# Turns between stages by token tile with a late scale, gathers for two expert pairs, and a last expert matrix loaded by halves of its columns

## The chip, the cores and the metric

One Trainium2 chip, of which the kernel uses one core. The metric is the device time of one execution in microseconds. PE is TensorE (matmul), ACT ScalarE, DVE VectorE, POOL GpSimd, SP the engine that issues the loads. SBUF is the on-chip memory, PSUM the eight banks that TensorE writes.

## The reference

Three layers over S = 256 tokens of width D = 1024, all in fp32. Layers 0 and 1 are each attention and a gated FFN with a convolution of three taps over the tokens (MLA attention in layer 0, differential attention in layer 1). The third has block and index attention and a mixture of 32 experts, two of which each token takes.

```python
# layers 0 and 1
a = rms_norm(h, norm_g[i, 0]);  a = mla_mixer(...) or diff_mixer(...)
h = h + rms_norm(a, norm_g[i, 1])
f = conv_ffn(rms_norm(h, norm_g[i, 2]), ...)   # up 1024 -> 2 x 2816, conv, gelu(g) * val, down
h = h + rms_norm(f, norm_g[i, 3])
# third layer: attention as above, then for each expert e and the tokens routed to it
hid = jax.nn.silu(xb @ w1[e]) * (xb @ w3[e])   # 1024 -> 512
ys = hid @ w2[e]                               # 512 -> 1024
```

rms_norm(x, g) is x * rsqrt(mean(x*x) + eps) * g, for each token.

## The kernel before

Tokens are held in two tiles of 128 (t = 0, 1): `h` and `xn` are 128 x 2 x 1024 in SBUF. The weights of layers 0 and 1 and of the third layer's attention come as pieces of 2048 columns through a ring of four raw buffers. ACT makes the high fp32r part of a piece (L1281), POOL the low part (`lows`, L611), and PE forms three fp32r products of each pair of operands (L649 to L651: high by high, low by high, high by low). A piece therefore passes SP, ACT and POOL before PE, in this order. Each engine runs a program of its own, in order, held together by semaphores. Instructions of one engine don't pass each other, so the place of an instruction in it is the schedule.

A stage's output goes to the next at a **turn**. There are four: from the MLA output projection to the FFN of layer 0 (turn 1, next input `x1`), from there to the differential attention (turn 2, `x2`), from that to the second FFN (turn 3, `x3`), and on to the third layer (turn 4, `x4`). In `post` DVE multiplies each of the four PSUM banks by the gain into `xn` (L1758), while ACT sums the squares (L1292), forms one scale for both tiles (L1764, then L1306 on ACT and L1683 to L1691 on DVE) and adds the scaled rows to `h` (L1770). At turns 1 to 3 ACT then squares `h`, DVE forms the next scale and writes `xn` with it (`normed`, L1734); PE transposes `xn` (L659), ACT copies the high part (L1323) and DVE makes the low part (L1710). At turn 4 the next scale isn't applied to `xn` (`x_gained`, L1746): it is put in as a row behind the first products. Meanwhile PE runs 32 matmuls that nobody uses, so that its clock stays up:

```python
WAIT = 32
```

In an FFN tile ACT centres the PSUM bank of the up product with its first tap and bias (L1458), DVE adds the other taps (L1931, L1936), ACT and DVE form the gelu, and DVE leaves the high and low hidden parts (L1945, L1947); PE uses them some tiles later in the down product. ACT splits the next piece between these steps.

In the expert stage 32 experts are taken in 16 pairs, 64 slots to an expert. Each expert has three matrices of 2 MB, which stay fp32 and come through slots of SBUF that earlier stages leave (`four_pairs`, L565 to L590; SP waits on `slots_used`). Per pair PE does w1 and w3 (L1211), the selection's transposes, the gather of the next pair's tokens (L1163), the transposes of the hidden part (L1222), w2 (L1237), and the scatter of the pair before (L1193). The gather multiplies `xn` with a 0/1 matrix `Sel` that DVE makes from the tokens' positions in their expert (L2197), and DVE copies it out (L2205). The last pair's w2 is loaded in two parts of its rows k.

## Time and profile before

| | us |
|---|---|
| median of 3 runs | 1363.15 |
| lowest and highest run | 1363.07, 1370.86 |
| profiled execution, its own time | 1361.37 |
| its span | 1359.6 |
| PE busy | 1285.8 (95%) |
| ACT busy | 549.0 (40%) |
| POOL busy | 568.2 (42%) |
| DVE busy | 510.5 (38%) |
| bytes moved | 341.22 MB |

The mean granted clock of PE was 0.992. The time is some 1.8 us more than the span of the engines' work. The three thirds of the span differ: up to 880 us the engines share the work of split weights, from about 906 us the transfers stand at 428 GB/s with POOL idle, and the last 25 us are the end of the last pair and the final norm. Parts of the page give shares over the whole span; the stretches are seen in the windows and timelines.

### The profile page before, as it was taken

How to read it: one execution, taken by the hardware profiler on the slowest of the kernel's cores; microseconds unless marked ns; L12 is line 12 of the kernel's file. 1: busy time of each engine (PE TensorE's matmuls, PEld its weight loads, DVE VectorE, ACT ScalarE, POOL GpSimd, SP SyncE). 2: the span in 40 equal slices, each digit the busy share in tenths (PEclk: the TensorE clock that was granted, in tenths of full speed). 3: DMA queues.
4: the chain of work that ended last, by engine and by line, in shares of the span. 5: the costliest groups of instructions: out<-in, count | busy, mean ns of one | idle time of the engine just before them, and what ended most of it. 6: DMA issues, size and time to landing. Idle time of an engine off the chain costs nothing.

```text
span 1359.6 us, 20047 instructions
## 1 busy us (share of the span) xinstructions
PE 1285.8 (95%) x7971; PEld 958.3 (70%) x7971; DVE 510.5 (38%) x1307; ACT 549.0 (40%) x853; POOL 568.2 (42%) x132
## 2 busy tenths in 40 slices
PE   6999999999998899999999899999999999999996
PEld 5867899998986799999877788854445444454442
DVE  2334544445265454444657264431112111121113
ACT  4544655556477465555544465221111111111112
POOL 5532788885954188888568555400000000000000
PEclk9999999999999999999999899999999999999998
DMA  7622566654633176665446443599999999999994
GB/s 268 216 81 89 154 199 200 190 187 154 217 124 94 62 213 190 186 185 172 154 147 201 135 145 128 208 422 426 429 429 428 428 428 430 429 430 429 429 427 176
DMA packets 154821, 341.22 MB, mean 251 GB/s; under 512 B 8473, under 2 KB 119418, under 8 KB 142202
## 3 DMA queue, kind: packets, MB, share of 16 engines
q1 hardware_dynamic: 154746, 340.18, 67.2%
q8 instruction: 53, 0.87, 0.3%
q14 instruction: 22, 0.18, 0.0%
HBM read 339.10 MB, written 1.05 MB: 250 GB/s over the span
## 4 chain that ended last, share of the span: by engine, by line
PE 72%; DMA 15%; DVE 5%; ACT 4%; POOL 2%; issue 2%; SPq 0%; ACTq 0%; DVEq 0%
PE bank L649 16%; PE bank L651 15%; PE bank L650 15%; DMA ring<-in_w 10%; PE bank L1211 10%; PE bank L1237 5%; DMA xspare<-in_w 4%; PE bank L1163 2%; PE bank L748 2%; POOL parts L611 2%; PE bank L659 1%; ACT parts L1281 1%; PE bank L1193 1%; PE bank L1097 1%; PE bank L782 1%
## 5 line engine op out<-in xcount | busy, mean ns | idle before, releaser
L611 POOL TENSOR_TENSOR parts<-raw,parts 128x2048 fp32r<-128x2048 f32 (+4 forms) x128 | 568.0, 4465 | 305.5 <-ACT parts L1281 305.5
L649 PE MATMUL bank<-xh,parts 128*128 128x256 f32 x1032 | 289.0, 280 | 12.1 <-ACT room L1318 5.9
L650 PE MATMUL bank<-xl,parts 128*128 128x256 f32 x1032 | 286.7, 278 | 0.0
L651 PE MATMUL bank<-xh,parts 128*128 128x256 f32 x1032 | 286.6, 278 | 0.0
L1281 ACT ACTIVATE parts<-raw 128x2048 fp32r<-128x2048 f32 (+4 forms) x128 | 235.9, 1853 | 33.1 <-PE bank L649 18.0
L1211 PE MATMUL bank<-ring,room 128*64 128x512 f32 x768 | 226.2, 594 | 8.6 <-DMA ring<-in_w 5.8
L649 PEld LDWEIGHTS bank<-xh,parts 128*128 128x128 f32 x1032 | 194.5, 189 | 18.9 <-issue 10.6
L650 PEld LDWEIGHTS bank<-xl,parts 128*128 128x128 f32 x1032 | 195.3, 189 | 0.8
L651 PEld LDWEIGHTS bank<-xh,parts 128*128 128x128 f32 x1032 | 194.6, 189 | 0.0
L1211 PEld LDWEIGHTS bank<-ring,room 128*64 128x64 f32 x768 | 73.3, 137 | 112.5 <-issue 112.5
L649 PE MATMUL bank<-parts,xh 128*128 128x512 f32 (+5 forms) x304 | 114.6, 377 | 9.6 <-POOL parts L611 2.8
L1237 PE MATMUL bank<-ring,room 128*64 128x512 f32 x384 | 113.3, 595 | 0.7 <-ACT room L1642 0.7
L650 PE MATMUL bank<-parts,xh 128*128 128x512 f32 (+5 forms) x304 | 112.0, 368 | 0.0
L651 PE MATMUL bank<-parts,xl 128*128 128x512 f32 (+5 forms) x304 | 112.0, 368 | 0.0
L1642 ACT ACTIVATE room<-bank 128x512 f32<-128x512 f32 x16 | 9.6, 597 | 193.6 <-PE bank L1222 193.6
L651 PE MATMUL bank<-parts,hl 128*128 128x512 f32 x192 | 75.6, 394 | 0.0
L649 PE MATMUL bank<-parts,hh 128*128 128x512 f32 x192 | 74.6, 389 | 0.8 <-POOL parts L611 0.8
L650 PE MATMUL bank<-parts,hh 128*128 128x512 f32 x192 | 75.3, 392 | 0.0
L1458 ACT ACTIVATE room<-bank,room 128x256 f32<-128x256 f32 x64 | 32.7, 561 | 102.2 <-PE bank L651 101.1
L649 PEld LDWEIGHTS bank<-parts,xh 128*128 128x128 f32 x304 | 57.9, 190 | 22.4 <-issue 4.9
L1318 ACT ACTIVATE room<-bank 128x512 f32<-128x512 f32 (+1 forms) x75 | 41.1, 581 | 77.3 <-PE bank L659 35.2
L1237 PEld LDWEIGHTS bank<-ring,room 128*64 128x64 f32 x384 | 34.5, 137 | 50.2 <-issue 48.0
(255 smaller groups left out, 1804.4 us busy)
## 6 DMA issues: line engine op xcount, KB each, us to landing
ring<-in_w SPq DMA_DIRECT2D x71, 2048.0 KB, 23.1
raw<-in_ffn_w_up SPq DMA_DIRECT2D x88, 512.0 KB, 4.9
room<-in_w SPq DMA_DIRECT2D x12, 2048.0 KB, 20.1
raw<-in_ffn_w_down SPq DMA_DIRECT2D x44, 512.0 KB, 3.9
xspare<-in_w SPq DMA_DIRECT2D x11, 2048.0 KB, 26.8
raw<-in_w_in SPq DMA_DIRECT2D x40, 512.0 KB, 4.2
raw<-in_diff_w_qkv SPq DMA_DIRECT2D x24, 512.0 KB, 4.5
raw<-in_mla_w_o SPq DMA_DIRECT2D x8, 512.0 KB, 4.6
```

Source lines behind the costliest of these rows:

```text
L611: pool.tensor_tensor(low[:, p % PARTS, 0:n], raw[:, p % RING, 0:n], high[:, p % PARTS, 0:n], ALU.subtract).then_inc(low_ready, 1)
L649: first = pe.matmul(out_, a[0], b[0], start=start, stop=False)
L650: pe.matmul(out_, a[0], b[1], start=False, stop=False)
L651: return first, pe.matmul(out_, a[1], b[0], start=False, stop=stop)
L659: ins = pe.transpose(b[0:cols, at:at + rows], src, ident[0:rows, 0:rows])
L748: ins = pe.matmul(b[:, t * S:t * S + S], qs[n][:, t * P:t * P + P], ks[n], start=n == 0, stop=n == len(qs) - 1)
L1163: ins = pe.matmul(bank[2 + k // 4][:, P * (k % 4):P * (k % 4) + P], xn[:, t, P * k:P * k + P], Sel[:, t].rearrange("p e c -> p (e c)"), st ...
L1211: ins = pe.matmul(bank[x][CAP * e:CAP * e + CAP, :], XgT[:, k, CAP * e:CAP * e + CAP], rows_of(j, x, e, k, EF), start=k == 0, stop=k == KT ...
L1237: ins = pe.matmul(bank[1 + hf][CAP * e:CAP * e + CAP, :], hidT[:, k, CAP * e:CAP * e + CAP], rows_of(j, 2, e, k, D)[:, 512 * hf:512 * hf + ...
L1281: act.activation(high[:, p % PARTS, 0:n], raw[:, p % RING, 0:n], ACT.Copy).then_inc(high_ready, 1)
L1318: act.activation(dst, src, func, scale=scale).then_inc(bank_moved[BANK[g]], 1)
L1458: act.activation(fbuf[b][a], bank[b][:, a * S:a * S + S], ACT.Identity, bias=par(3, a), scale=par(1, a)).then_inc(centre, 1)
```

## The change

It has three parts. **The turns** (`turn_over` for `post`, `normed` and `x_gained`): DVE takes the two token tiles one after the other, in halves of 512 columns, each tile with a scale of its own; POOL makes the second halves of `xn`; the next rms scale isn't applied to `xn` at turns 1 to 3 either, but is formed after the transposes, put on the diagonal of a matrix by DVE and turned into a row over all tokens by two small PE matmuls (`scales_in_rows`) behind the first group of products. In the FFN DVE multiplies each up tile in PSUM by this row ahead of the centring; the q and k groups of the differential attention are multiplied by it as they are copied out, by DVE instead of ACT; v takes the scale in ACT's copy. `WAIT` is 8. **The experts**: the rows are split into fp32r high (ACT) and low (DVE), `Sel` holds four experts and is double buffered, and a gather step fills half the rows of the input for two pairs, with 16 fp32r matmuls over 256 columns a pair instead of 16 fp32 ones over 128. **The last w2** is loaded and used by halves of its columns.

In the order of the diff below: POOL's gains, PE's fillers, scale row and gathers, ACT's `x_next`, DVE's `turn_over`, FFN tile and rows' split, and SP's last loads.

```diff
+            def gains(site):
+                pool.wait_ge(gpre_here, 16 * (site + 1))
+                for t in range(NT):
+                    pool.wait_ge(h_ready, 2 * (site - 1) + t + 1)
+                    pool.tensor_tensor(xn[:, t, 512:D], h[:, t, 512:D], gpre[:, 512:D], ALU.mult).then_inc(xn_ready, 1)
+            next_stage = {W[name] + 1: n + 1 for n, name in enumerate(["ffn0", "qkv", "ffn1", "qi"])}
...
-            WAIT = 32
+            WAIT = 8
...
+            def scales_in_rows(n):
+                pe.wait_ge(diag_ready, n)
+                g = G[f"row{n}" if n < 4 else "row"]
+                b = begin(g)
+                for t in range(NT):
+                    ins = pe.matmul(b[:, t * P:t * P + P], cs[:, C_ONE:C_ONE + P], diag[:, t], start=True, stop=True)
...
                 up(b, 0)
+                scales_in_rows(2 * l + 1)
                 up(b + 1, 1)
...
+            def gather(half, at, first, last, sel, b=2, frees=0):
                 for k in range(first, last):
+                    for x in range(2):
+                        for t in range(NT):
+                            row = (row_high[t], rows_r[:, t, :])[x][:, P * (at + k):P * (at + k) + P]
+                            ins = pe.matmul(bank[b + k // 2][:, 2 * P * (k % 2):2 * P * (k % 2) + 2 * P], row,
+                                            Sel[sel][:, t].rearrange("p e c -> p (e c)"),
...
             def one_round(base, fours, first=False, behind=None):
-                gather(base)
+                pe.wait_ge(sel_ready, 2 + base)
+                gather(base, 0, 0, 4, 0)
+                gather(base + 1, 4, 0, 4, 0, b=4)
...
+            def x_next(site):
+                high_tiles(f"x{site}", HALVES, 4)
+                h_sums(site, 28, 8448)
+                if site < 4:
+                    g = G[f"row{site}"]
+                    full(act, g)
+                    if site == 2:
+                        act.activation(late_key_row, bank[BANK[g]][:, 0:S], ACT.Copy, scale=HD_SCALE).then_inc(key_row, 1)
+                    copy(g, late_row, bank[BANK[g]][:, 0:S])
...
+                for t in range(NT):
+                    scale_of(t)
+                    added(t, 0)
+                    dve.tensor_tensor(xn[:, t, part[0]], h[:, t, part[0]], gpre[:, part[0]], ALU.mult).then_inc(xn_ready, 1)
+                for t in range(NT):
+                    added(t, 1)
+                late_scales(name, site + 1)
...
             def tile(n, b, par):
+                dve.wait_ge(up_full, 1 + n)
+                both = bank[b][:, :].rearrange("p (a s) -> p a s", a=2)
+                dve.tensor_tensor(both, both, late_row.unsqueeze(1).to_broadcast([P, 2, S]), ALU.mult).then_inc(rows_put, 1)
...
+            for t in range(NT):
+                dve.wait_ge(rows_high, t + 1)
+                dve.scalar_tensor_tensor(rows_r[:, t, :], xn[:, t, :], st[:, 16 + t:17 + t],
+                                         row_high[t], ALU.mult, ALU.subtract).then_inc(rows_split, 1)
             dve.wait_ge(mask_ready, 1)
...
-                            sp.dma_start(slots[c][:, a * HALF:a * HALF + HALF].unsqueeze(1),
-                                         w[:, bass.ds(8 * i + (2 * j + e), 1), a * HALF:a * HALF + HALF]).then_inc(done[c], 16)
+                            sp.dma_start(r3(slots[c], b=D)[:, :, 512 * a:512 * a + 512],
+                                         A["w2_2"][0].rearrange("e (p k) n -> p e k n", p=P)[
+                                             :, 8 * i + 2 * j + e, :, 512 * a:512 * a + 512]).then_inc(done[c], 16)
```

DVE's program at turn 1, before:

```order
L1758 TENSOR_TENSOR xn<-bank,gpost 128x512 x4
L1764 TENSOR_TENSOR st<-st 128x2
L1683 TENSOR_SCALAR st<-st 128x1 x2
L1688 TENSOR_SCALAR st<-st 128x1 x2
L1691 TENSOR_SCALAR st<-st 128x1 x2
L1770 SCALAR_TENSOR_TENSOR h<-xn,st,h 128x1024 x2
L1683 TENSOR_SCALAR st<-st 128x1 x2
L1688 TENSOR_SCALAR st<-st 128x1 x2
L1691 TENSOR_SCALAR st<-st 128x1 x2
L1734 SCALAR_TENSOR_TENSOR xn<-h,st,gpre 128x512 x4
L1710 TENSOR_TENSOR xl<-bank,xh 128x4x128 x4
```

and now:

```order
L1806 TENSOR_TENSOR xn<-bank,gpost 128x512
L1815 TENSOR_TENSOR st<-st 128x1
L1806 TENSOR_TENSOR xn<-bank,gpost 128x512
L1736 TENSOR_SCALAR st<-st 128x1
L1741 TENSOR_SCALAR st<-st 128x1
L1744 TENSOR_SCALAR st<-st 128x1
L1826 SCALAR_TENSOR_TENSOR h<-xn,st,h 128x512
L1835 TENSOR_TENSOR xn<-h,gpre 128x512
```

The two gains, the scale and half an addition of one tile stand together now; tile 1 repeats the eight rows, and after them come two more halves of `h`, the low parts, and only then the scale of the next norm and its diagonal:

```order
L1826 SCALAR_TENSOR_TENSOR h<-xn,st,h 128x512 x2
L1763 TENSOR_TENSOR xl<-bank,xh 128x4x128 x4
L1736 TENSOR_SCALAR st<-st 128x1 x2
L1741 TENSOR_SCALAR st<-st 128x1 x2
L1744 TENSOR_SCALAR st<-st 128x1 x2
L1789 COPY st<-st 128x2
L1792 TENSOR_SCALAR room<-cs,st 128x128 x2
L1997 TENSOR_TENSOR bank<-bank,room 128x512
L2000 SCALAR_TENSOR_TENSOR room<-bank,convT,room 128x255 x2
```

ACT's program at turn 2 (`x2`), before, from the scale of `h` to the first split pieces:

```order
L1306 ACTIVATE st<-st,eps_t 128x2
L1323 ACTIVATE xh<-bank 128x4x128 x4
L1499 ACT_TABLE_LOAD
L1499 ACTIVATE st<-st 128x2
L1281 ACTIVATE parts<-raw 128x2048 x2
L1318 ACTIVATE room<-bank 128x512
L1281 ACTIVATE parts<-raw 128x2048
L1318 ACTIVATE room<-bank 128x512
```

and now:

```order
L1359 ACTIVATE st<-st,eps_t 128x1
L1376 ACTIVATE xh<-bank 128x4x128 x4
L1345 ACTIVATE room,st<-h 128x1024 x2
L1359 ACTIVATE st<-st,eps_t 128x2
L1550 ACTIVATE prow<-bank 128x256
L1371 ACTIVATE room<-bank 128x256
L1561 ACT_TABLE_LOAD
L1561 ACTIVATE st<-st 128x2
L1334 ACTIVATE parts<-raw 128x2048 x7
```

The squaring of `h` has moved behind the copies of the transposed tiles, the two row copies (L1550, L1371) stand ahead of the table load (L1561), and the seven splits (L1334) stand behind all of them with no copy of q or k between.

DVE's program at the head of the experts, before:

```order
L2177 TENSOR_SCALAR room<-room 128x2
L2182 SCALAR_TENSOR_TENSOR room<-bank,room 128x64
L2184 TENSOR_SCALAR room<-room 128x64
L2185 TENSOR_REDUCE st<-bank 128x1
L2187 TENSOR_SCALAR flag<-st 128x1
L2197 TENSOR_TENSOR room<-cs,room 128x128 x2
```

and now:

```order
L2251 TENSOR_SCALAR room<-room 128x2
L2254 SCALAR_TENSOR_TENSOR rows_r<-xn,st,gains_r 128x1024
L2254 SCALAR_TENSOR_TENSOR rows_r<-xn,st,tables_r 128x1024
L2260 SCALAR_TENSOR_TENSOR room<-bank,room 128x64
L2262 TENSOR_SCALAR room<-room 128x64
L2263 TENSOR_REDUCE st<-bank 128x1
L2265 TENSOR_SCALAR flag<-st 128x1
L2273 TENSOR_TENSOR room_r<-cs,room 128x256 x2
```

The two low parts of the rows (`rows_r`) stand ahead of the positions, and the selection (L2273) is twice as wide.

## Rows read from the trace of the kernel before

**Rows 1.** Page, part 4, the chain that ended last, share of the span by engine.

```profile
PE 72%; DMA 15%; DVE 5%; ACT 4%; POOL 2%; issue 2%; SPq 0%; ACTq 0%; DVEq 0%
```

**Rows 2.** Windows; columns: window, us, busy of each engine, PEclk, DMA share, GB/s.

```profile
210.00:300.00 90.00, 90.00 (x648) 84.09 (x648) 43.12 (x104) 49.36 (x62) 77.11 (x18) 1.00 0.61 190
...
904.00:906.00 2.00, 2.00 (x10) 0.72 (x12) 1.21 (x6) 0.38 (x1) 0.00 (x0) 1.00 0.98 336
906.00:1335.00 429.00, 418.50 (x2268) 200.54 (x2266) 75.75 (x162) 55.07 (x75) 0.00 (x0) 1.00 1.01 428
```

**Rows 3.** The chain that ended last, in order of time; columns: start us, us, what.

```profile
1298.29 31.55 DMA ring<-in_w
...
1339.59 7.11 PE bank L1237 x32
...
1348.07 1.47 DVE h L2232 x3
```

**Rows 4.** Timeline around turn 2, and its last FFN tile; columns: start, us, engine, line, operation.

```profile
315.48 0.42 DVE L1947 TENSOR_TENSOR hl<-bank,hh 128x256 fp32r<-128x256 f32 x1
...
319.27 2.68 DVE L1758 TENSOR_TENSOR xn<-bank,gpost 128x512 f32<-128x512 f32 x4 [3.37 <-ACT room L1292]
...
320.11 7.24 PEld L678 LDWEIGHTS bank<-xh 128*128 128x128 f32 x32
...
323.32 2.48 DVE L1770 SCALAR_TENSOR_TENSOR h<-xn,st,h 128x1024 f32<-128x1024 f32 x2
...
332.29 0.19 PEld L649 LDWEIGHTS bank<-xh,parts 128*128 128x128 f32 x1 [0.80 <-DVE xl L1710]
...
332.38 1.28 ACT L1499 ACT_TABLE_LOAD   x1
...
334.07 3.70 ACT L1281 ACTIVATE parts<-raw 128x2048 fp32r<-128x2048 f32 x2
...
338.25 0.60 ACT L1318 ACTIVATE room<-bank 128x512 f32<-128x512 f32 x1 [0.47 <-PE bank L651]
...
343.90 0.60 ACT L1318 ACTIVATE room<-bank 128x512 f32<-128x512 f32 x1 [3.25 <-PE bank L651]
```

**Rows 5.** Timeline of turn 4.

```profile
651.92 7.25 PEld L678 LDWEIGHTS bank<-xh 128*128 128x128 f32 x32
...
657.52 2.49 DVE L1746 TENSOR_TENSOR xn<-h,gpre 128x512 f32<-128x512 f32 x4
...
662.06 0.19 PEld L649 LDWEIGHTS bank<-parts,xh 128*128 128x128 f32 x1 [0.96 <-DVE xl L1710]
```

**Rows 6.** Timeline of turn 1 and of the FFN's first pieces behind it.

```profile
125.09 7.23 PEld L678 LDWEIGHTS bank<-xh 128*128 128x128 f32 x32
...
143.22 1.02 ACT L1458 ACTIVATE room<-bank,convT 128x256 f32<-128x256 f32 x2 [5.89 <-PE bank L651]
...
150.75 0.38 PE L649 MATMUL bank<-xh,parts 128*128 128x256 f32 x1 [1.92 <-POOL parts L611]
```

**Rows 7.** The widest form of POOL's low parts; count, busy us, mean ns, idle before.

```profile
L611 POOL TENSOR_TENSOR parts<-raw,parts 128x2048 fp32r<-128x2048 f32 x116 | 533.7, 4627 | 277.7 <-ACT parts L1281 277.7
```

**Rows 8.** Timeline of POOL and of DVE around 711.

```profile
708.67 9.67 POOL L611 TENSOR_TENSOR parts<-raw,parts 128x2048 fp32r<-128x2048 f32 x2 [9.08 <-ACT parts L1281]
...
711.20 2.67 DVE L2045 TENSOR_TENSOR score<-score,cs 128x512 f32<-128x512 f32 x1
```

**Rows 9.** Windows where the clock fell, and one where it held.

```profile
449.00:451.00 2.00, 0.87 (x4) 0.69 (x5) 0.75 (x1) 0.29 (x1) 2.00 (x1) 0.97 0.00 0
451.00:453.00 2.00, 2.00 (x6) 1.61 (x5) 0.00 (x0) 0.50 (x2) 2.00 (x1) 0.50 0.00 0
742.00:746.00 4.00, 1.32 (x10) 0.87 (x9) 3.90 (x8) 3.98 (x3) 2.46 (x1) 1.00 0.42 145
```

**Rows 10.** Timeline of the head of the experts.

```profile
891.50 0.22 DVE L2182 SCALAR_TENSOR_TENSOR room<-bank,room 128x64 f32<-128x64 f32 x1 [1.32 <-PE bank L1151]
...
892.91 3.81 PE L1163 MATMUL bank<-room,xn 128*128 128x128 f32 x32 [1.52 <-DVE room L2197]
```

More of the change, by code:

```diff
@@ L249, in build @@
         h = sb("h", [P, NT, D])
+        with nc.sbuf_tensor("rows_r", [P, NT, D], F32R) as rows_r:
+            pass
         xn = sb("xn", [P, NT, D])
@@ L998, in _ @@
             by_token(G["qi"], W["qi"], X, [3, 3, 2], [256, 328])
-            pe.wait_ge(diag_ready, 1)
-            b = begin(G["row"])
-            for t in range(NT):
-                ins = pe.matmul(b[:, t * P:t * P + P], cs[:, C_ONE:C_ONE + P], diag[:, t], start=True, stop=True)
-                if t == 0:
-                    behind(ins)
-            end(ins, G["row"])
+            scales_in_rows(4)
             columns("qa")
@@ L1949, in ffn @@
             def ffn(l):
+                moved(dve, G[f"row{2 * l + 1}"])
                 for j in range(6):
@@ L2219, in pair @@
                                          ALU.mult).then_inc(hidden_ready, 1)
-                if not last:
-                    take(n + 1)
+                if gathers:
+                    take(n + 2, j % 2, (j // 2 + 1) % 2)
                 for hf in range(2):
@@ L2251, in _ @@
             link(ins)
-            link(dve.tensor_copy(gpair, gate[:, :, 0:2]))
-            take(0)
+            gates_of(0).then_inc(gates_put, 1)
+            for half in range(2):
+                take(half, half, 0, 2 + 2 * half)
             dve.wait_ge(flag_ready, 1)
@@ L2262, in _ @@
                     dve.wait_ge(last_added, 4 * r)
-                    select(r * NP, 0)
-                    take(r * NP)
+                    select(0, 0)
+                    gates_of(0).then_inc(gates_put, 1)
+                    for half in range(2):
+                        take(r * NP + half, half, 0, 2 + 2 * half)
                     one_round(r * NP)
```

295 lines of the change are left out of this document (158 added, 137 removed).

## The prediction

> **What bounds the kernel now.** I read the chain that ended last first: TensorE has 72% of it and DMA 15% [rows 1]. The windows say where each holds. In the loops of the conv-FFN TensorE is busy for all 90 of 90 us, in the expert stage (906 to 1335) the DMA share is 1.01 at 428 GB/s [rows 2]. The end of the chain confirms the second: the last w3 of a pair lands at 1329.84 after 31.55 us, and only then TensorE goes on [rows 3]. The expert stage moves 32 experts of 6.3 MB, 201.3 MB; at 428 GB/s that is 470 us, so its length is fixed by when its stream starts and how it ends, not by TensorE. Between the two stand the four turns, where TensorE has only its filler (L678). With T the filler's first weight load, the first product of the next stage follows at T+12.18 in turn 2 (320.11 to 332.29) and T+10.14 in turn 4 (651.92 to 662.06) [rows 4, 5]. Turn 1 has the same T+12.2, but there TensorE runs dry again later: ACT splits the third piece of the FFN only behind the first tile's centring (L1458, 143.22), POOL needs 4.6 us more, and TensorE resumes at 150.75, T+25.7 with T = 125.09 [rows 6]. Turn 3 has the same shape.
>
> **The change, part by part.** All times below are against T of their turn.
>
> *1. The turn's own chain.* Before: four products with the gain, one scale for both tiles, two additions of 1024, two squarings of 1.06 us, a second scale, four xn, transposes [rows 4]. After: DVE does tile 0 to the end, then tile 1. Prices: 0.69 for a 128x512 pass (2.68 us for four), about 1.0 for the sum and scale of one tile (for two they lie between 321.95, where L1758 ends, and 323.32). Turn 2: DVE may start 0.8 before T (L1758 at 319.27). Tile 0: two gains, sum, scale, one half added, one half of xn: until T+2.8. Tile 1 the same again, 3.7: T+6.4 to 6.6. Two more additions: h is ready at T+7.1 and 7.8. Then POOL makes the second halves. It ran no 512-wide pass; 2048 wide took 4.63 us [rows 7], a quarter is 1.16, and I take 1.3 with something for the start. POOL: 7.2 to 8.5 to 9.8. Last transposes (0.66 a set) end at T+10.5, and the product begins there, since its first half of the tiles has been ready long since. I add 0.3 for DVE and POOL holding each other up, so T+10.8 in turns 2 and 4. Turns 1 and 3 have squares 1.4 us earlier: T+9.4.
>
> That 0.3 is a choice between 0 and 0.7. The row for it: an addition of 128x512 with both inputs in SBUF took 2.67 us at 711.20 while a POOL pass ran from 708.67 on [rows 8], and the same form takes 0.62 in turn 4, where POOL stands still [rows 5]. In the new turn POOL's two passes overlap at most the last addition and the first low parts, so one instruction can be late by up to half a POOL pass.
> The Trainium skill (SBUF — State Buffer, Who interferes with whom) says that a DVE instruction with two SBUF inputs contends with a GpSimd instruction that reads SBUF, and that whoever issues first keeps the shared ports for its whole length; this trace agrees, 2.67 against 0.62 us. By that rule and the estimate of 1.3 us a pass the sum would gain up to 1.3 us more per turn.
>
> *2. The fillers.* Eight instead of 32: they end at about T+2.1 instead of T+7.7. After that TensorE has only sets of four transposes in 6 to 7 us. What such a hole does stands in the windows: at 449:451 TensorE was busy 0.87 of 2 us, and at 451 the granted clock went to 0.50, the lower of its two levels; in 742:746, busy 1.32 of 4, it held [rows 9]. Either may follow the new holes. A fall costs what the half-speed stretch of some 3 to 3.5 us withholds, less what was idle in it: 0.2 to 1.9 us. I take 1.0 for each turn, as the chance of it is above even.
>
> *3. Turns 1 and 3.* Here the third piece decides, not the first product. First group of products: T+9.4, 5.9 long as in turn 2 (332.29 to the copy at 338.25), plus 1.0 of clock: T+16.3. Now the scale row stands between it and the centring: row product 0.5, ACT's copy 0.65, DVE's multiplication of the tile in PSUM 0.7; then centre 0.95, split 1.9, POOL 4.6. Sum: T+25.6, against T+25.7. Worth 0 each (-1.6 if the clock holds). What the shorter chain wins, the row and the multiplication spend.
>
> *4. Turn 2.* ACT's work behind it sets the end again, by a new order: all seven splits now stand behind both row copies, and behind the table load. T+10.8, first group 5.65, clock 1.0, row product 0.75: 18.2. Two copies 0.8, table and exp (1.28 and 0.2) 1.5, split 1.9, POOL 4.63: T+27.0. Before, the two splits of L1281 began at 334.07, within the first group, and the third group could start at T+12.2+2x5.65 = T+23.5. Worth +3.5 (+2.0 without the clock and the 0.3; +4.5 with more idle in a half-speed stretch).
>
> *5. Turn 4.* It had the late scale already, and a T of 10.14. After: 10.8 plus 1.0, so +1.6 (0 to +2.7).
>
> *6. The FFN tiles.* 44 multiplications of 0.69 us on DVE, 30 us of work. In the loops DVE is busy 43 of 90 us and TensorE all of it, so they cost nothing if the delay of 0.7 to 0.8 a tile fits. The tightest place is the last tile, which nothing follows: its low part is done at 315.90, and its twelve products of 0.23 us (L678: 7.24 for 32) end where the filler begins, at 320.3 [rows 4], so begin at 317.6. Slack 1.7: it fits. If the cover were gone, 44x0.7 is 31 us.
>
> *7. Head of the experts.* DVE's two new splits of the rows (128x1024, two SBUF inputs, 1.25 each by L1770) stand ahead of the positions, on which select and gather wait. DVE was idle for 1.32 us ahead of L2182 and hides that much of the 2.5: +1.2 [rows 10]. Select is 256 wide instead of 128: +0.4. Gather: 16 fp32 matmuls (32 records, two for each) took 3.81 us; two half gathers of 16 products over 256 columns, at the 0.117 us of such a product in the FFN (48 between the copies at 338.25 and 343.90, 5.65 us), are 1.87 each. They begin at 892.91+1.2+0.4 = 894.5 and end at 898.2; the experts' first product, at 896.7 before, comes 1.5 later. TensorE's idle ahead of the gather grows from 1.5 to about 2.9 us: another possible fall of the clock, +1.0 (0 to 1.7). Does the stream feel it? The loads that follow go into the room that the first matrix leaves, about 7 us behind the gather, and at 904:906 the rate is 336 GB/s [rows 2]: the stream is nearly dry there, so a later first matrix passes one to one. +2.5.
>
> *8. Gathers of two pairs.* 1.9 us a pair less on TensorE. A pair's 12.6 MB take 29.4 us at 428 GB/s, and TensorE was busy 418.5 of 429 us, at most 28.7 of each 29.4: it waits already, and with 1.9 less it waits longer: 0.
>
> *9. Last matrix by halves of columns.* Its first half now ends earlier, but the additions to h queue behind DVE's second low part and started at 1348.07 [rows 3]. Gain 0 to 0.3, I take 0.2. Rows of 2 KB instead of 8 KB could slow the load. By 428 GB/s its 4.2 MB end some 9.8 us behind the w3 before it, at 1339.7, and the second half is wanted half of L1237's 7.11 us after 1339.59, at 1343.1: 3 us of cover, 0.
>
> Sum: 0 + 3.5 + 0 + 1.6 + 2.5 - 0.2 = +7.4. The profiled execution took 1361.37, 1.8 below the median of 1363.15, so it would be 1368.8 there; on the median's scale 1370.5, which I round to 1370.
>
> **The rivals.**
> *A, the clock holds* in the turns and at the head, and contention costs nothing: -1.6-1.6+2.0+0+1.5-0.2 = +0.1: 1363. For it: 742:746 held. Against: 449:451 did not.
> *B, the turns' chain gains more* than I count (POOL's passes overlap better, ACT gets ahead of the table load): each turn 2 us shorter than forecast, 1355 to 1358. Faster by under 1%.
> *C, TensorE bounds the expert stage*: then 14 to 16 pairs by 1.9 give -27 to -30: about 1336 to 1340. Against it stands a DMA share of 1.01 over 429 us.
> *D, the FFN's multiplication is exposed.* It decides once the chain from a full bank to its low part (centre, convolution, gelu on ACT and DVE alternately) exceeds the slack of two tiles. Beyond it each 0.3 us a tile costs 13: 1380 to 1395.
>
> **How the numbers follow.** About 1% (13.6 us) is what a measurement of this kernel can tell from no change. Forecast 0.58, A 0.18, B 0.09, C 0.04, D and like stalls 0.11. Cases A, B and the forecast lie within 1%, but the forecast's upper end (all clock terms at 1.9, turn 2 at 4.5) reaches 1377: a little of it is slower. Faster 0.06, same 0.80, slower 0.14. The range leaves out C, D and part of B: 1358 to 1378.
>
> **What would show it.** Turn 2: first product at T+10.8 and a wait of TensorE for POOL's low part before the third group, ending at T+27; ACT's first split after the table load. Turns 1 and 3: resumption at T+25.6. PEclk at half in each turn. The first expert product 1.5 to 2.5 us later against the head's start, DMA share 1.01 behind it, and TensorE's wait per pair longer by 1.9. Wrong if TensorE idles between FFN tiles, if the experts' stream falls below 428 GB/s, or if no wait for POOL follows turn 2.

## The result, and the profile after

The change makes the kernel slower. The median is 1381.55 us (1380.13 to 1382.94, 4 runs) against 1363.11 (1361.99 to 1370.86); the ratio is 1.0135, 95% interval 1.0107 to 1.0162. The forecast was 1370, so about 7 of the 18 us were seen, and the rest was not. The interval excludes a difference of under 1%.

The page of the changed kernel, its first line, and the chain by engine, which answers to [rows 1]:

```profile
span 1379.8 us, 19410 instructions
...
PE 63%; DMA 21%; DVE 7%; ACT 4%; POOL 3%; issue 2%; SPq 0%; ACTq 0%; DVEq 0%; POOLq 0%
```

The cores view: span and mean granted clock. It was 0.992 before:

```profile
core 0: 1379.8 us, clock 0.969
```

The chain has lost TensorE's share to DMA and DVE, and the clock has lost 0.023. Multiplied out, (1 - mean clock) x span x 2 is the time at half speed: 86 us here, 22 before. That is the first thing to see.

Both kernels run the same 4680 split products ahead of the experts, and the same 1024 of w1 and w3 in them. The n-th one of each trace can therefore be set side by side, and the growth of its delay shows where the 20.2 us of span arose:

| place | delay grows by | forecast |
|---|---|---|
| turn 1, with the stretch behind its late third piece | +1.8 | 0 |
| last tile of the first FFN | +1.0 | 0 |
| turn 2 and its q, k and v products | +4.2 | +3.5 |
| differential attention | +4.3 | 0 |
| turn 3, with the stretch behind its late third piece | +0.7 | 0 |
| last tile of the second FFN | +1.0 | 0 |
| turn 4 | +1.1 | +1.6 |
| attention of the third layer | +3.5 | 0 |
| head of the experts | +3.0 | +2.5 |
| experts and end | -0.4 | -0.2 |

Six rows with a forecast of 0 hold 12.3 us. The windows show the other common cause. Columns are window, us, busy of each engine, PEclk, DMA share, GB/s, for the changed kernel:

```profile
131.00:138.00 7.00, 5.67 (x26) 5.27 (x27) 3.14 (x9) 3.63 (x8) 2.39 (x2) 0.52 0.00 0
329.00:336.00 7.00, 5.03 (x22) 4.23 (x23) 4.37 (x7) 2.85 (x6) 2.87 (x2) 0.52 0.28 67
349.00:352.00 3.00, 2.19 (x10) 2.19 (x11) 0.00 (x0) 1.51 (x1) 3.00 (x2) 0.57 0.34 90
414.00:421.00 7.00, 6.06 (x23) 4.86 (x24) 2.85 (x6) 1.72 (x6) 2.96 (x1) 0.52 0.42 120
...
756.00:759.00 3.00, 1.02 (x8) 0.58 (x8) 2.90 (x6) 3.00 (x2) 1.36 (x1) 1.00 0.58 204
760.00:766.00 6.00, 6.00 (x15) 4.65 (x15) 2.53 (x5) 2.74 (x9) 6.00 (x2) 0.51 0.46 149
926.00:1355.00 429.00, 401.75 (x2012) 176.31 (x2010) 73.45 (x146) 55.07 (x75) 0.00 (x0) 0.98 1.01 427
```

There are half-speed stretches in turn 1 (131), turn 2 (329), behind the late pieces (349), in the differential attention (414), and in the third layer's attention (760), where the kernel before kept its clock through the same hole at 742 [rows 9]. Up to the first gather of the experts the trace has thirteen such stretches, the trace of before three. Those three stand ahead of the same products here too (at 442, 462 and 779); ten are new, of which five were forecast. The last row answers to [rows 2]: the expert stage still runs at a DMA share of 1.01, with TensorE busy for 402 instead of 418 of 429 us. What the wider gathers save is idle time.

**Turn 2** in the changed kernel's timeline, which answers to [rows 4]. Its T is the first filler's weight load:

```profile
322.86 1.80 PEld L715 LDWEIGHTS bank<-xh 128*128 128x128 f32 x8
...
330.27 2.87 POOL L642 TENSOR_TENSOR xn<-h,gpre 128x512 f32<-128x512 f32 x2 [6.96 <-DVE h L1826]
...
333.96 0.56 PE L686 MATMUL bank<-xh,parts 128*128 128x256 f32 x1
...
341.14 0.38 ACT L1550 ACTIVATE prow<-bank 128x256 f32<-128x256 f32 x1 [3.80 <-PE bank L840]
...
341.82 1.28 ACT L1561 ACT_TABLE_LOAD   x1
...
343.23 5.50 ACT L1334 ACTIVATE parts<-raw 128x2048 fp32r<-128x2048 f32 x3
...
345.20 18.26 POOL L633 TENSOR_TENSOR parts<-raw,parts 128x2048 fp32r<-128x2048 f32 x4 [12.07 <-ACT parts L1334]
...
349.81 0.58 PE L686 MATMUL bank<-xh,parts 128*128 128x256 f32 x1 [3.25 <-POOL parts L633]
```

The first product comes at T+11.1 (forecast T+10.8), the third group at T+26.95 (forecast T+27.0) behind a wait of 3.25 us for POOL. And ACT stands idle for 3.80 us ahead of the row copies, with two pieces waiting to be split behind them.

**The last tile of the first FFN**, DVE and ACT and then the product that waits:

```profile
313.26 0.42 DVE L2016 TENSOR_TENSOR hl<-bank,hh 128x256 fp32r<-128x256 f32 x1
313.60 0.69 DVE L1997 TENSOR_TENSOR bank<-bank,room 128x512 f32<-128x512 f32 x1
...
314.33 1.02 ACT L1511 ACTIVATE room<-bank,room 128x256 f32<-128x256 f32 x2 [2.36 <-DVE bank L1997]
...
319.75 0.42 DVE L2016 TENSOR_TENSOR hl<-bank,hh 128x256 fp32r<-128x256 f32 x1
...
320.23 0.50 PE L686 MATMUL bank<-parts,hh 128*128 128x512 f32 x1 [0.72 <-DVE hl L2016]
```

The low part that was done at 315.90 before [rows 4] is done at 320.17. Of these 4.3 us, 1.75 is the delay that TensorE has throughout the FFN's loop, so the tile itself is 2.5 us later, against a slack of 1.7. The multiplication takes 0.69 us, but it stands behind the whole of the tile before on DVE, and ACT's centring can't start ahead of it any more.

**The differential attention.** The changed kernel's DVE and PE at one step:

```profile
411.68 0.69 DVE L2044 TENSOR_TENSOR room<-bank,prow 128x512 f32<-128x512 f32 x1 [0.78 <-PE bank L688]
...
414.11 0.69 DVE L2060 TENSOR_TENSOR room<-bank,rs_o 128x512 f32<-128x512 f32 x1
...
414.94 2.05 PE L811 MATMUL bank<-room 128*128 128x128 f32 x8 [2.87 <-DVE room L2060]
```

and the same step before:

```profile
405.83 0.69 DVE L1981 TENSOR_TENSOR room<-bank,rs_o 128x512 f32<-128x512 f32 x1
...
406.66 1.13 PE L774 MATMUL bank<-room 128*128 128x128 f32 x8 [1.59 <-ACT room L1318]
```

DVE now copies a k group out (L2044), and waits for TensorE's own products to do so, ahead of the scale and the scaling of two heads' outputs (L2060). TensorE waits 2.87 us for them, then the clock is at half: its eight matmuls take 2.05 instead of 1.13 us.

**Head of the experts**, which answers to [rows 10]:

```profile
907.71 1.28 DVE L2254 SCALAR_TENSOR_TENSOR rows_r<-xn,st,gains_r 128x1024 fp32r<-128x1024 f32 x1
908.91 1.28 DVE L2254 SCALAR_TENSOR_TENSOR rows_r<-xn,st,tables_r 128x1024 fp32r<-128x1024 f32 x1
910.10 0.22 DVE L2260 SCALAR_TENSOR_TENSOR room<-bank,room 128x64 f32<-128x64 f32 x1
...
911.78 0.36 PE L1212 MATMUL bank<-room_r,gains_r 128*128 128x256 f32 x1 [2.76 <-DVE room_r L2273]
```

The idle time ahead of the gather is 2.76 us (forecast 2.9), and the clock falls at 913, within the gather.

Executions of one kernel differ by more than these terms: the kernel before ran between 1358.0 and 1371.6 in 63 executions. So each verdict below rests on several executions or on a place in a trace, and the text says on which. The changed kernel itself was timed in one set alone; the kernel before had a median of 1361.3 beside e1 to e4, 1363.3 beside e9 to e12 and 1363.2 beside e13 to e16. The four sets of experiments ran on four chips. A distance to the changed kernel's 1381.55 therefore compares two sets, and is uncertain by some 2 us.

### The profile page after: what moved, and what is told of

The parts are those of the page before. It is cut to its first block, busy times and chain, and to the rows that moved or that the text cites. A ratio compares the mean times of both kernels' runs of the same rounds, so it can differ in the third digit from the quotient of the medians.

```text
span 1379.8 us, 19410 instructions
## 1 busy us (share of the span) xinstructions
PE 1269.4 (92%) x7631; PEld 935.6 (68%) x7631; DVE 558.1 (40%) x1358; ACT 546.8 (40%) x853; POOL 579.1 (42%) x140
## 4 chain that ended last, share of the span: by engine, by line
PE 63%; DMA 21%; DVE 7%; ACT 4%; POOL 3%; issue 2%; SPq 0%; ACTq 0%; DVEq 0%; POOLq 0%
DMA ring<-in_w 16%; PE bank L686 15%; PE bank L688 15%; PE bank L687 15%; PE bank L1262 7%; DMA xspare<-in_w 4%; PE bank L1289 3%; PE bank L785 2%; POOL parts L633 2%; ACT parts L1334 1%; PE bank L696 1%; POOL xn L642 1%; PE bank L1212 1%; DVE h L1826 1%; PE bank L1145 1%
## 5 line engine op out<-in xcount | busy, mean ns | idle before, releaser
L686 PE MATMUL bank<-xh,parts 128*128 128x256 f32 x1032 | 293.8, 285 | 15.7 <-POOL parts L633 9.4
L687 PE MATMUL bank<-xl,parts 128*128 128x256 f32 x1032 | 290.4, 281 | 0.0
L688 PE MATMUL bank<-xh,parts 128*128 128x256 f32 x1032 | 290.2, 281 | 0.0
L1334 ACT ACTIVATE parts<-raw 128x2048 fp32r<-128x2048 f32 (+4 forms) x128 | 235.5, 1852 | 49.3 <-PE bank L686 28.4
L1262 PE MATMUL bank<-ring,room 128*64 128x512 f32 x768 | 232.8, 609 | 17.4 <-DMA ring<-in_w 13.1
L686 PEld LDWEIGHTS bank<-xh,parts 128*128 128x128 f32 x1032 | 198.9, 193 | 22.0 <-issue 10.6
L687 PEld LDWEIGHTS bank<-xl,parts 128*128 128x128 f32 x1032 | 198.9, 193 | 0.8
L688 PEld LDWEIGHTS bank<-xh,parts 128*128 128x128 f32 x1032 | 198.5, 192 | 0.0
L1262 PEld LDWEIGHTS bank<-ring,room 128*64 128x64 f32 x768 | 75.5, 140 | 125.1 <-issue 125.1
L686 PE MATMUL bank<-parts,xh 128*128 128x512 f32 (+5 forms) x304 | 116.9, 385 | 8.4 <-DVE room L1867 2.7
L1289 PE MATMUL bank<-ring,room 128*64 128x512 f32 x384 | 113.3, 596 | 1.7 <-DMA ring<-in_w 1.0
L687 PE MATMUL bank<-parts,xh 128*128 128x512 f32 (+5 forms) x304 | 113.9, 375 | 0.0
L1289 PEld LDWEIGHTS bank<-ring,room 128*64 128x64 f32 x384 | 35.1, 137 | 50.9 <-issue 47.5
L2298 DVE SCALAR_TENSOR_TENSOR room<-room,bank 128x512 f32<-128x512 f32 x16 | 18.1, 1128 | 124.2 <-PE bank L1262 124.2
```

The source lines that it names most:

```text
L686: first = pe.matmul(out_, a[0], b[0], start=start, stop=False)
L687: pe.matmul(out_, a[0], b[1], start=False, stop=False)
L688: return first, pe.matmul(out_, a[1], b[0], start=False, stop=stop)
L1262: ins = pe.matmul(bank[x][CAP * e:CAP * e + CAP, :], XgT[j // 2 % 2][:, k, P * (j % 2) + CAP * e:P * (j % 2) + CAP * e + CAP], rows_of(j, ...
L1289: ins = pe.matmul(bank[1 + hf][CAP * e:CAP * e + CAP, :], hidT[:, k, CAP * e:CAP * e + CAP], rows_of(j, 2, e, k, D)[:, 512 * hf:512 * hf + ...
L1334: act.activation(high[:, p % PARTS, 0:n], raw[:, p % RING, 0:n], ACT.Copy).then_inc(high_ready, 1)
```

## The experiments

All but e3, e4, e11 and e12 are edits of the changed kernel.

**e1, 32 fillers again.**

```diff
-            WAIT = 8
+            WAIT = 32
```

> The changed kernel with 32 fillers at each turn again instead of 8 (nothing else). Theory 'clock': a good part of the 20 us lies in stretches at half clock, of which 131 to 138, 328 to 336, 475 to 480 and 670 to 678 begin in the turns after the eight fillers. With 32 the fillers end at T+7.7 and the last two sets of transposes are not due before T+7 to T+10, so these four stretches go away or shrink and the span falls by 3 to 6 us, to 1374 to 1377. Rival 'place in the program': the lost time comes from the order on ACT and DVE; then the span stays within 1 us of 1379.8, or grows by up to 1 us a turn, since the first transposes now queue behind the fillers.

One execution, 1383.7 us, 2.2 more than the changed kernel, not 3 to 6 less. In its trace two stretches at half clock don't belong to the edit, one at 40 us (+1.5) and one at 720 (+3.2, of which 2.2 come back at 760 and 780, where its stretches are shorter). At the turns themselves, each up to its third piece, the delay falls by 0.8, 0.6 and 1.0 us in turns 1, 2 and 4 and grows by 0.3 in turn 3. The first product comes 1.0 us later behind the longer filler in turns 1 and 3 and 0.3 to 0.4 earlier in the other two, and the first group then runs at full clock in all four. So in this trace fillers at this place are worth 2.1 us in sum; the time of a single execution can't show that.

**e2, fillers between the transposes.**

```diff
+            BETWEEN = (5, 3, 1)
                 for q in range(2):
                     for t in range(NT):
+                        if site:
+                            keep_busy((0, BETWEEN[0], BETWEEN[1], BETWEEN[2])[2 * q + t], begin(G[name] + 2 * q + t))
                         pe.wait_ge(xn_ready, 4 * site + 2 * q + t + 1)
```

> The changed kernel with fp32 fillers of 256 columns on constants put between the sets of transposes of the four turns: 5, 3 and 1 of them ahead of sets 2, 3 and 4. They fill TensorE's idle time of 2.1 to 2.7, 1.3 to 1.8 and 0.5 us without being in the way. Theory 'clock': no half-speed stretch begins within a turn, first products come 0.5 us earlier, the first group of products takes 5.7 instead of 6.9 us, together 4 to 7 us less: 1375 to 1378 as time. Rival 'place in the program': nothing changes but 0.3 us a turn. Either way the stretches behind the late third piece (151, 349) stay, since their holes are not filled.

1375.15 us, 5 executions, ratio to before 1.0099 (1.0064 to 1.0135). By the ratios (1.0135 - 1.0099) that is 4.9 us less than the changed kernel, by the medians 6.4, within the range of "clock"; the two intervals overlap, so the size is loose. The stretches in the four turns are gone. Time at half clock, by the median execution, is 58 instead of 86 us. Up to the third piece of each turn the delay falls by 1.8, 0.8, 0.7 and 1.1 us, 4.4 in sum; the rest lies in later stretches that are shorter in this trace.

**e3, the kernel before with eight fillers.**

```diff
-            WAIT = 32
+            WAIT = 8
```

> The kernel before with only the number of fillers changed, 8 for 32. The old turn leaves TensorE idle from T+2 to T+9. Theory 'clock': a half-speed stretch in each of the four turns, each worth 1 to 2 us of the products behind it: +4 to +8 us. Rival: the clock is a matter of the whole stage and eight fillers do as well: within 1 us.

1369.9 us, 10 executions, ratio 1.0055 (1.0033 to 1.0078): some 7.5 us, within the expected 4 to 8. Windows of its turns 1 and 2:

```profile
133.00:140.00 7.00, 5.42 (x27) 5.30 (x28) 6.12 (x12) 2.39 (x4) 0.00 (x0) 0.53 0.00 0
331.00:338.00 7.00, 5.61 (x27) 5.49 (x28) 6.41 (x13) 3.68 (x5) 0.00 (x0) 0.53 0.34 112
```

The clock was 1.00 there before. The cut of the fillers has its price without any other part of the change.

**e4, the kernel before with the experts' part alone.** The edit is the change's diff from `gather` on, with `rows_split` and the last w2.

> The kernel before with the expert part of the change alone (rows split in high and low, gathers for two pairs, last w2 by halves of columns); the turns and their 32 fillers as before. Prediction's step: the first expert product 1.5 us later, another 1.0 if the clock falls in the idle time ahead of the gather, nothing gained on the way, so +1.3 to +2.8 us in all; the half-speed stretch would stand at about the first gather. Rival 'TensorE bounds the expert stage': 14 to 16 pairs by 1.9 us, -27 to -30. Rival 'the stream catches up': 0, since loads wait in a full ring.

1367.4 us, 10 executions, ratio 1.0040 (1.0022 to 1.0058), which is 3.0 to 7.9 us; expected were 1.3 to 2.8. In its trace the head is 3.0 us later against the attention, in place of the expected 1.5 to 2.5, and the half-speed stretch stands at 892, about the first gather. "TensorE bounds the expert stage" (-27) is refuted, and "the stream catches up" too: the delay to before is 0.0 at the first expert product and 0.0 again at the last w3. In the middle of the stage TensorE runs up to 7 us ahead of the kernel before. Behind the last w3 this execution loses another 1.8 us that the expected sum has no term for: DVE stands idle ahead of the final norm, and the profile shows nothing that it waited for.

```profile
1352.45 2.50 DVE L2304 TENSOR_TENSOR xn<-h,gpost 128x512 f32<-128x512 f32 x4 [1.99 <-issue]
```

No other trace has this idle time, and whether it came in the other nine executions isn't known.

**e5, the FFN's multiplication of every tile in the middle of the tile before.**

```diff
                 dve.scalar_tensor_tensor(fbuf[b][2], u[0], 1.0, x[0], ALU.add, ALU.mult).then_inc(g_inner, 1)
+                if not last:
+                    put_row(n + 1, (b + 1) % 4)
```

> The changed kernel, but in the FFN DVE multiplies the next tile's bank by the scale row already in the middle of a tile (behind its first gelu product, where it waits for the tanh), instead of at the head of its own tile. Theory 'order': the last tile's low part comes 4.3 us later than before because its multiplication (313.60) stands behind the whole work of the tile before, so ACT's centring starts at 314.33 instead of 309.56; hoisted, both FFNs end without a wait for the last tile, shift 1.6 and 1.4 us less: the gap ahead of the last twelve products (0.72 <-DVE hl at 320.23) is gone. Rival 'too much work': DVE's 0.69 a tile itself is the cause; then the gap stays at 0.7 or TensorE waits elsewhere in the loop. Span 1376 to 1378 by the first, 1379 to 1381 by the second, with 2 us more or less for stretches at half clock that come and go between executions.

One execution, 1390.1, a miss. The last twelve products of both FFNs come 1.0 us earlier, not 1.6 and 1.4; by the table above 1.0 is all that there was to gain. For an even tile DVE now waits up to 5.6 us for the bank, since TensorE fills two tiles and then does a down product. And in the second FFN every product over 256 columns took 3.7% longer at a granted clock of 1.00 (last section), 4.1 us in sum, which has nothing to do with the expectation. Inconclusive on the sum; e13 does it for every second tile.

**e6 and e14, outputs ahead of the q/k copy.**

```diff
-                if s in (1, 3, 5):
-                    two_heads(G[f"diff_q{s}"], QKV[5 + s])
                 if s in (5, 7, 9, 11):
                     outputs_scaled((s - 5) // 2)
                 elif s in (6, 8, 10):
                     outputs_low(s // 2 - 3)
+                if s in (1, 3, 5):
+                    two_heads(G[f"diff_q{s}"], QKV[5 + s])
```

> The changed kernel, but in the differential attention DVE scales the outputs of a pair of heads first and copies the next q or k group out behind it (only the order of these two at one step changes). Theory 'order': at 411 to 415 TensorE waits 2.87 us for L2060, which stands behind the new L2044 and its wait for TensorE's own products; a half-speed stretch of 6.8 us follows. With the order turned round the shift there falls from +3.5 to about +1 us. Rival: TensorE's wait is the clock's doing alone; then it stays. Span 1376 to 1378 by the first.

> The same kernel as e6, timed: outputs scaled ahead of the q/k copy at one step of the differential attention. The look gave -4.1 us at this place and -5.1 in the end: median 1376 to 1378 if it is the order, above 1380 if the look was a lucky execution.

1376.5 in one execution, 1376.2 as the median of 4 in a second set (ratio to before 1.0107, 1.0059 to 1.0154): 5.4 us less than the changed kernel by the medians, 3.8 by the ratios, whose intervals overlap. The place shows it better. In both traces 3.5 to 3.7 us go at one product, the 2184th, and 4.1 to 4.3 within four: exactly where the delay had grown by 3.5 and 4.1. The order of two helpers at one step cost all of that, the half-speed stretch of 6.8 us included.

**e7 and e15, splits ahead of the scale row.**

```diff
                 h_sums(site, 28, 8448)
+                if site == 1:
+                    split(W["ffn0"] + 2)
+                if site == 2:
+                    split(W["qkv"] + 3)
+                if site == 3:
+                    split(W["ffn1"] + 2)
                 if site < 4:
```

> The changed kernel, but at turns 1 to 3 ACT splits the next one or two pieces while it waits for the scale row, instead of behind the row's copy. Theory 'order': the third group at turn 2 (+3.7 us and 0.8 of clock) and the third piece of the FFN at turns 1 and 3 (waits of TensorE for POOL's low part up to 150.9 and 493.2, each followed by a half-speed stretch) are late only by ACT's place in its program; all three waits for POOL L633 go, 4.5 + 2 + 2 us less: span 1370 to 1373. Rival 'POOL': POOL's 4.6 us from the turn on are what is late; then the waits shrink by less than half, span above 1376.

> The same kernel as e7, timed: splits ahead of the scale row's copy at turns 1 to 3. The look gave -1.9, -3.7 and -2.5 us at the three turns, less a stretch at 39 that does not belong to it: median 1372 to 1375 if these hold, above 1379 if not.

1376.4 in one execution; 1374.8 as the median of 8 executions (ratio 1.0079, 1.0054 to 1.0105), 6.8 us less than the changed kernel by the medians, 7.6 by the ratios. ACT and POOL at turn 2 in e15:

```profile
335.83 3.71 ACT L1334 ACTIVATE parts<-raw 128x2048 fp32r<-128x2048 f32 x2
340.39 0.38 ACT L1556 ACTIVATE prow<-bank 128x256 f32<-128x256 f32 x1 [0.85 <-PE bank L840]
...
337.81 13.78 POOL L633 TENSOR_TENSOR parts<-raw,parts 128x2048 fp32r<-128x2048 f32 x3 [6.09 <-ACT parts L1334]
```

ACT's idle time ahead of the row copies is 0.85 instead of 3.80 us, POOL starts 7.4 us earlier, and the waits for it at the third piece are gone in all three turns. The stretches behind the third pieces are gone with them. At turn 1 2.9 of the 5.6 us gained are given back at the next pieces, at turn 3 2.6 of 3.4. "POOL itself is late" is refuted.

**e8, the rows' low part by halves.**

```diff
+            rows_low(0)
             dve.wait_ge(mask_ready, 1)
...
             select(0, 0)
+            rows_low(1)
```

> The changed kernel, but DVE makes the low part of the first 512 columns of the rows ahead of the positions and that of the others behind the selection, for the second half gather. Theory 'order': the head was 3.0 us late because 2.5 us of splits stand ahead of the positions and the idle time (2.76 us) brought a half-speed stretch at 912; with half of it hidden in DVE's idle 1.3 us the first expert product comes 1.2 to 2.5 us earlier and all behind it too: span 1377 to 1378.5. Rival 'the stream absorbs it': first product earlier, end unchanged.

One execution, 1382.2, a miss of the whole, with the step itself within what was expected. Two windows of its trace and the first gather:

```profile
903.00:910.00 7.00, 7.00 (x27) 6.28 (x26) 3.80 (x24) 4.50 (x8) 0.00 (x0) 0.52 0.99 419
910.00:914.00 4.00, 2.21 (x16) 1.95 (x16) 2.75 (x9) 0.87 (x6) 0.00 (x0) 1.00 1.03 442
...
913.76 0.36 PE L1212 MATMUL bank<-room_r,gains_r 128*128 128x256 f32 x1 [1.79 <-DVE room_r L2278]
```

The idle time ahead of the gather is 1.79 instead of 2.76 us, and from the last small product of the positions to the first expert product it takes 6.0 instead of 8.5 us. But in this execution the clock fell ten us earlier, through the router's products, and took 2.9 us there.

**e9, the four repairs of order together; e10, with fillers.** e9 joins e14, e15, e8 and the multiplication of every second tile ahead. e10 adds e2 and ten fillers ahead of the first gather.

> The changed kernel with the four repairs of order and none of the clock: q and k groups behind the outputs' scaling, pieces split ahead of the scale row's copy at turns 1 to 3, every second FFN tile's multiplication ahead of its turn, the rows' low part by halves. Theory 'order and clock each hold about half': order alone takes 6 to 12 us off the changed kernel's 1381.5 (TensorE's waits for POOL at 151, 349 and 493, for the last FFN tiles at 320 and 662, and for L2060 at 415 go, with the half-speed stretches behind them); the stretches at 131, 329, 476, 670, 759, 779 stay: 1369 to 1376. Theory 'clock alone': over 1378.

> The same with the fp32 fillers between the transposes of the turns and ten more fillers ahead of the first gather. The stretches at 131, 329, 476, 670 and 912 go as well, 5 to 8 us more than order alone: 1359 to 1368, at the level of the kernel before (1361.3). If the clock does not matter, the same as order alone within 1.5 us.

e9: 1365.4 us, 10 executions, ratio 1.0014 (0.9993 to 1.0034). It can't be told from the kernel before, and is 16 us below the changed one, more than expected. The four edits alone sum to some 10 us by their medians (e14 5.4, e15 6.8, e13 and e8 nothing), so 6 of the 16 aren't accounted for singly. A part shows behind turn 1, where e9 gives back 0.8 us of what its early split gains, and e15 2.9. e10: 1355.3 us, 11 executions, ratio 0.9942 (0.9924 to 0.9959), 10 us less again and faster than before, where 1359 to 1368 was expected. Time at half clock, by the median execution: 74 us in e9, 38 in e10. The profiled execution of e10 at turn 1, and around the diff attention's step:

```profile
131.00:138.00 7.00, 6.24 (x45) 5.17 (x44) 3.59 (x9) 4.33 (x9) 2.86 (x2) 1.00 0.00 0
...
412.00:419.00 7.00, 7.00 (x37) 5.56 (x36) 5.22 (x19) 6.94 (x22) 0.84 (x1) 1.00 0.53 150
```

**e11, the turns alone; e12, the turns repaired, experts as before.** e11 is the kernel before with the change's turns and eight fillers. e12 is e11 with e2, e14, e15 and the multiplication of every second tile ahead.

> The kernel before with the change's turns, scale rows and eight fillers, but the experts' rows, gathers and last w2 as before. By the shifts of the trace the turns and what hangs on them hold +17.6 of the 20.2 us up to 898, the head of the experts +3.0: 1375 to 1380, three us below the changed kernel's 1381.5; half-speed stretches in the expert stage are gone, and that gives nothing beyond the 3 us if the stage is bound by its loads.

> The turns of the change with their three repairs of order and the fillers, experts as before. Three us less than the repaired kernel with the experts' part if that part only costs (1356 to 1364); it then beats both kernels. If the experts' part had become worth something on this ground, the difference to the run with it is under 1 us.

e11: 1380.7 us, 4 executions, ratio 1.0112 (1.0069 to 1.0155), 0.7 above the expected 1375 to 1380 and only 0.8 below the changed kernel; the intervals hold 3 us as well. Its trace has 1.6 us from a stretch at 40 and 4.1 us of slow pace in the first FFN (last section), neither of which belongs to the edit. e12: 1355.0 us, 11 executions, ratio 0.9939 (0.9919 to 0.9958). It beats both kernels, and e10 equals it: with its head repaired the experts' part costs nothing that can be measured, and brings nothing.

**e13, every second FFN tile ahead.**

```diff
-                    tile(l * FT + j, j % 4, lambda w, a: convT[:, l, w, a, j:j + 1])
+                    tile(l * FT + j, j % 4, lambda w, a: convT[:, l, w, a, j:j + 1], first=j % 2 == 0, last=j % 2 == 1)
```

> The changed kernel with every second FFN tile multiplied by the scale row in the middle of the tile before (its bank is full by then, which the next even tile's is not: that cost DVE waits of 6 us for TensorE in e5). Theory 'order': TensorE's waits ahead of the last twelve products of both FFNs (0.7 us at 320, and the rest of the 1.6 and 1.4 us of shift) go, 2.5 to 3.5 us: 1378 to 1379 median. Rival: part is given back at the turn behind, since the first product of turn 2 came at the same time in e5: 1380 to 1381.

1383.1 us, 4 executions (1381.3 to 1385.8; ratio 1.0143, 1.0104 to 1.0182), no gain and outside what was expected. Its DVE at the end of the first FFN:

```profile
310.44 0.70 DVE L1995 TENSOR_TENSOR bank<-bank,room 128x512 f32<-128x512 f32 x1 [0.98 <-PE bank L688]
...
312.74 0.86 DVE L2004 SCALAR_TENSOR_TENSOR room<-bank,room 128x255 f32<-128x255 f32 x2
...
317.10 0.43 DVE L2022 TENSOR_TENSOR hl<-bank,hh 128x256 fp32r<-128x256 f32 x1
```

The low part is done at 317.5 instead of 320.2, and TensorE's wait is gone; the delay falls by 1.0 us at the end of each FFN, which is the whole of the two rows. In the second FFN the products over 256 columns are slower by 3.7% again and cost 4.1 us (last section). So the cause of these 1.0 us is shown, and the worth of the repair alone isn't.

**e16, the last w2 by rows.** Loaded by halves of its rows, used by halves of columns.

```diff
-                            sp.dma_start(r3(slots[c], b=D)[:, :, 512 * a:512 * a + 512],
+                            sp.dma_start(slots[c][:, a * HALF:a * HALF + HALF].unsqueeze(1),
...
-                    if hf and by_halves:
-                        pe.wait_ge(second_half, 32)
                     for k in range(4):
+                        if k == 2 and not hf and by_halves:
+                            pe.wait_ge(second_half, 32)
```

> The changed kernel with the last w2 again loaded by halves of its rows k (8 KB pieces) but used by halves of columns. Prediction: no difference by more than 0.3 us, since the load lands about 3 us before its second half is wanted: from the last w3's first product to the end of the last w2's products 17 us in both, DMA idle at the same distance. Rival: rows of 2 KB are slower to load; then the changed kernel's end would be 1 us or more later than this one's, counted from the last w3.

One execution, 1382.6. From the last w3's first product to the first scatter product of the second half it takes 18.21 us in both traces. The 2 KB rows cost nothing here, and gain nothing.

## Why the prediction was wrong

The side was wrong (slower by over 1% had a chance of 0.14) and so was the range, by 3.6 us. Three steps failed: the clock's reach (part 2), the slack of the last FFN tile (part 6), and the differential attention, which stands in no part. Against the profiled execution's +7.4 the span grew by 20.2, so 12.8 us were not seen. Stretches behind the late third pieces hold 4.5 of them, the last FFN tiles 2.0, the differential attention 4.3 and the third layer's attention 3.5; the rest came 1.5 us smaller than forecast. Step by step:

- **What bounds the kernel: right.** The expert stage stayed at a DMA share of 1.01, and what the gathers save became waiting (e4). Rival C was refuted.
- **Parts 1 and 5, the turn's chain: right.** First products at T+9.2, 11.1, 9.2 and 10.6 against 9.4, 10.8, 9.4 and 10.8. POOL's two passes took 2.87 us, 0.3 more than estimated; the first of them began while DVE's last addition still ran. The Trainium skill (SBUF — State Buffer, Who interferes with whom) has whoever issues first keep the shared ports and the other wait. The trace fits, as the addition took its usual 0.7 us and the excess is on POOL's side, but no run here shows that apart.
- **Parts 3 and 4, the late third piece: right in place and time** (T+25.9 and T+27.0 in turns 1 and 2 against T+25.6 and T+27.0; turn 3, said to have turn 1's shape, came at T+24.8). What follows was missing. TensorE waited 3.1 to 3.2 us in each for POOL, and the clock fell again behind that (151, 349, 493), for another 1.6, 1.4 and 1.4 us. The step said that the splits stand behind the row copies, and took this as given; e15 shows that it was worth 7 us.
- **Part 6, the FFN tiles: failed.** "The delay of 0.7 to 0.8 a tile" counted the new instruction's length and not its place. On DVE it stands behind all of the tile before, so ACT's centring lost its head start, and the last tile came 2.5 us later against a slack of 1.7: +1.0 us in each FFN. The loops themselves hid it, as said.
- **Not in the sum at all: the differential attention, +4.3.** The change moved q and k copies from ACT to DVE; the prediction has no price for their 0.69 us and didn't ask what stands behind them. At one step it is the scaling that TensorE waits for. e14 shows all of it.
- **Part 2, the clock: right in kind, too small in reach.** One fall of 1.0 us per turn and one at the head were counted, five in all, and all five came. Five more did too: one behind each of the three waits for a third piece, one behind the wait of 2.87 us in the differential attention, and one in the third layer's attention. The 3.5 us of this last are of the clock alone: the hole at 756 is the one at 742, the instructions are the same, and this time the clock fell at 759, for 2.8 us. (The stretch at 779 is the one that the kernel before has at 761; it reaches further here, for 0.6.) e16, whose turns and attention are the changed kernel's, kept its clock there and had these 2.8 us less. Whether this fall is chance stays open: 13 of the 15 traces with the new turns have it (all but e10 and e16), and none of the three with the old ones. The fillers alone were worth 7.5 us on the old turns (e3) and 5 to 10 on the new ones (e2, e10 against e9).
- **Part 7, the head: right,** +3.0 against 2.5; the longer idle time behind DVE's splits and the fall of the clock both show. (Its own terms give 1.5 + 1.2 + 0.4 = 3.1 us of idle time and not 2.9; it was 2.76.) **Part 9: right** in that 2 KB rows cost nothing (e16); experts and end together gave 0.4 against 0.2.

By the runs, order on ACT and DVE with the falls that hang on it is worth 16 of the 18 us (e9). Fillers between the transposes and ahead of the gather give another 10 (e10 against e9), which is more than was lost: the kernel with both is faster than the one before by 8 us (5.6 to 10.4 by the interval), and e12 puts this gain on the turns.

## What to carry to other kernels

An instruction inserted on an in-order engine costs its length only if nobody waits for what stands behind it; list, for every place where one is put, the next instruction of that engine that another engine waits for, and what it itself waits for first. An operation that waits for a late input belongs behind the work that is ready (here the splits ahead of the row copy, the outputs ahead of the q/k copy). And when TensorE's filler is cut because the turn is shorter, look at the holes that are left between the pieces of real work: they may have to be filled too, or the next products can run at half speed (e3, e2).

## What the runs showed of the hardware that was not expected

- **The clock makes the spread.** Twenty executions of the kernel before on one chip had spans of 1358.3 to 1369.8 us and between 16 and 38 us at half clock; a straight line through them gives 0.54 us of span for each us at half clock. The same hole in the same program brought a fall in one execution and none in another (a stretch at 40 us stood in e1, e7, e8, e11, e15 and e16, and not in the others, with the same instructions up to there; e6 and e14 are one kernel, and e6 alone has a stretch at 436).
- **The expert stage forgives it.** The changed kernel's clock fell four times between 1076 and 1284, as TensorE idles more there, and the delay at the end was no larger than at the start. Behind the last load it doesn't: in e9 (1346) and e15 (1353) the clock fell within the last w2, and the delay grew by 1.6 us to the end.
- **A slower pace at full granted clock.** In e5, e9, e13 and e16 every product over 256 columns of the second FFN took 0.1178 instead of 0.1136 us, in e11 every one of the first FFN; those over 512 columns kept their 0.229. Here are the windows of the changed kernel and of e13, whose FFN differs in DVE's order alone:

```profile
520.00:640.00 120.00, 120.00 (x874) 112.58 (x874) 71.33 (x149) 65.29 (x82) 101.50 (x23) 1.00 0.64 192
```

```profile
520.00:640.00 120.00, 120.00 (x856) 112.75 (x856) 62.98 (x145) 64.49 (x80) 98.89 (x22) 1.00 0.63 188
```

874 products against 856 in the same 120 us, with TensorE busy throughout and PEclk 1.00. It costs 4 to 5 us an FFN. DVE's order isn't the cause, since e16 has the changed kernel's FFN unchanged and shows the slow pace too. The two kernels that were profiled twice (e6 and e14, e7 and e15) had the usual pace both times. Whether it belongs to the program or to the execution stays open.
